# Output gate's columns of the input projection in two groups of four banks, recurrent heads' preparation beside them, convolutions beside k's and v's columns

## The reference

```python
x = x + 0.5 * swiglu(rmsnorm(x), w1_gate, w1_up, w1_down)      # D_FF = 5504
proj = rmsnorm(x) @ w_in                                       # 7192 columns
q_a, k_a, v_a, f_a, qk_m, v_m, o_m, i_m, f_m = split(proj)
y_a = rmsnorm(forgetting_attention(q_a, k_a, v_a, f_a, paged cache))       # 8 heads of 128
qk_c = silu(causal_conv(qk_m, conv_prev))                      # 4 taps, 2048 channels
h_m, C, n, m = mlstm(q_m, k_m, v_m, i_m, f_m, C0, n0, m0)      # 8 heads of 128
y_m = sigmoid(o_m) * rmsnorm(h_m)
x = x + concat(y_a, y_m) @ w_out
x = x + 0.5 * swiglu(rmsnorm(x), w2_gate, w2_up, w2_down)
```

## Time and profile before

| | |
|---|---|
| median of 3 runs | 2315.3 us (2314.76 to 2317.62) |
| profiled execution | 2320.72 us |
| its span | 2319.1 us |
| PE, share of the span | 2290.2 us, 99% |
| DVE, ACT, POOL | 1228.4 us (53%), 842.8 us (36%), 50.3 us (2%) |
| mean granted TensorE clock | 0.994 |
| chain of waits | PE 95%, DVE 3%, ACT 1% |

### The profile page before, as it was taken

How to read it: one execution, slowest core, us unless ns; L and a number is a source line. 1 busy time by engine, 2 the same in 40 slices (tenths; PEclk the granted TensorE clock), 3 DMA queues, 4 the chain that set the end, 5 groups by cost and what they waited for, 6 DMA issues and landing times.

```text
span 2319.1 us, 48002 instructions
## 1 busy us (share of the span) xinstructions
PE 2290.2 (99%) x17805; PEld 2246.8 (97%) x17805; DVE 1228.4 (53%) x1907; ACT 842.8 (36%) x1109; POOL 50.3 (2%) x84
## 2 busy tenths in 40 slices
PE   9999999999999999999999999999999999999998
PEld 8999999999999999887999989999999999999997
DVE  6554444355444455467456766755554434554443
ACT  4333333333333343334334433533333333333332
POOL 2000000000000010010000110000000000000000
PEclk9999999999999999999999999999999999999999
DMA  6555555555554444547445455455554445555443
GB/s 169 180 166 164 164 164 175 166 166 163 171 166 166 165 152 146 168 136 271 157 164 167 132 155 173 151 181 163 163 163 168 171 168 169 168 164 168 164 163 131
DMA packets 176901, 384.05 MB, mean 166 GB/s; under 512 B 19133, under 2 KB 44853, under 8 KB 176501
## 3 DMA queue, kind: packets, MB, share of 16 engines
q1 hardware_dynamic: 173888, 375.99, 50.4%
q0 software_dynamic: 2512, 5.57, 0.8%
q10 hardware_dynamic: 416, 1.32, 0.2%
HBM read 373.09 MB, written 9.70 MB: 165 GB/s over the span
## 4 chain that ended last, share of the span: by engine, by line
PE 95%; DVE 3%; ACT 1%; DMA 0%; issue 0%; SPq 0%; POOL 0%; ACTq 0%; DVEq 0%; POOLq 0%
PE ps L1788 30%; PE ps L1786 30%; PE ps L1787 29%; DVE w_lo L1010 1%; PE ps L2044 1%; DMA w_raw<-in_w_up 0%; ACT w_hi L632 0%; PE ps L2057 0%; PE ps L1856 0%; PE ps L1857 0%; PE ps L1863 0%; PE ps L1990 0%; PE ps L2337 0%; PE ps L1979 0%; PE ps L2245 0%
## 5 line engine op out<-in xcount | busy, mean ns | idle before, releaser
L1010 DVE TENSOR_TENSOR w_lo<-w_raw,w_hi 128x1024 fp32r<-128x1024 f32 (+2 forms) x698 | 789.7, 1172 | 983.9 <-ACT w_hi L632 982.5
L632 ACT CAST w_hi<-w_raw 128x1024 fp32r<-128x1024 f32 (+2 forms) x698 | 670.6, 1008 | 1290.3 <-PE ps L1788 1284.7
L1786 PE MATMUL ps<-x_hi,w_hi 128*128 128x288 f32 (+1 forms) x2752 | 813.0, 295 | 4.4 <-DVE w_lo L1010 2.6
L1788 PE MATMUL ps<-x_hi,w_lo 128*128 128x288 f32 (+1 forms) x2752 | 813.9, 296 | 0.0
L1787 PE MATMUL ps<-x_lo,w_hi 128*128 128x288 f32 (+1 forms) x2752 | 807.7, 293 | 0.0
L1786 PEld LDWEIGHTS ps<-x_hi,w_hi 128*128 128x128 f32 x2752 | 517.5, 188 | 6.3 <-DVE w_lo L1010 3.0
L1787 PEld LDWEIGHTS ps<-x_lo,w_hi 128*128 128x128 f32 x2752 | 521.2, 189 | 0.1
L1788 PEld LDWEIGHTS ps<-x_hi,w_lo 128*128 128x128 f32 x2752 | 516.5, 188 | 0.0
L1786 PE MATMUL ps<-hid_hi,w_hi 128*128 (+1 forms) x1376 | 405.6, 295 | 1.4 <-DVE X L1243 1.4
L1788 PE MATMUL ps<-hid_hi,w_lo 128*128 (+1 forms) x1376 | 407.0, 296 | 0.0
L1787 PE MATMUL ps<-hid_lo,w_hi 128*128 (+1 forms) x1376 | 403.8, 293 | 0.0
(11 more groups left out here) (487 smaller groups left out, 1438.1 us busy)
## 6 DMA issues: line engine op xcount, KB each, us to landing
w_raw<-in_w_down SPq DMA_DIRECT2D x178, 512.0 KB
w_raw<-in_w_gate SPq DMA_DIRECT2D x320, 256.0 KB
w_raw<-in_w_up SPq DMA_DIRECT2D x320, 256.0 KB
w_raw<-in_w_in SPq DMA_DIRECT2D x64, 512.0 KB
w_raw<-in_w_in SPq DMA_DIRECT2D x64, 384.0 KB
page<-in_cache_k SPq DMA_DIRECT2D x16, 512.0 KB, 4.6
w_raw<-in_w_out SPq DMA_DIRECT2D x16, 512.0 KB
w_raw<-in_w_gate SPq DMA_DIRECT2D x32, 192.0 KB
```

Source lines behind the costliest of these rows:

```text
L632: nc.scalar.copy(w_hi[:, slot, 0:width], w_raw[:, slot, 0:width]).then_inc(w_hi_ready, 1)
L1010: nc.vector.tensor_tensor(w_lo[:, slot, 0:width], w_raw[:, slot, 0:width], w_hi[:, slot, 0:width].bitcast(F32), ALU.subtract).then_inc(w_l ...
L1786: mm(out, hi, x_hi[:, k, :], start=first and pair == 0 and s == slots[0], stop=False)
L1788: ins = mm(out, lo, x_hi[:, k, :], start=False, stop=last and pair == 1 and s == slots[-1])
```

## The change

`in_m` keeps three groups (q, k, v). The gate's columns become `in_o`: two groups of four banks (0 to 3), each with four turns of 512 columns, so that banks 4 to 7 are free meanwhile. The preparation of the heads moves in between: on PE `beside_o1` and `beside_o2` put its pieces after given banks of given pairs ("steps" 0 to 7 of each group), on DVE and ACT a loop over 16 steps puts the copies and weights behind each `split_o`. Only the first scores stay behind the columns. The convolutions move one group up, beside k's and v's columns, in the turns of k's columns 0, 2, 3 and 3 of them. The memory of the heads is laid out anew so that what is written early lies where input blocks are used up: `O_HALF` and `O_MOST` are the marks at which four and six of the last group's eight pairs are done. `qw` is made by POOL instead of DVE, the sigmoid is split in two halves (the second after the first head's exponential), `kws` and `vws` move to `xt`, `Ws` to `counts`, and the first state is loaded at `O_MOST`.

```diff
-    mixer = [("in_a", 4, KD, KD, plain[:6]), ("in_m", 4, KD, KD, plain),
+    mixer = [("in_a", 4, KD, KD, plain[:6]), ("in_m", 3, KD, KD, plain),
+             ("in_o", 2, KD, KD, plain[:4]),
...
+    kws, vws = (xt[:, i, 0:H * SM].rearrange("p (h s) -> p h s", s=SM) for i in range(2))
+    C_ring = [C0[:, :, :], C1[:, :, :]] + [w_raw[:, i, :].rearrange("p (b e) -> p b e", b=NB) for i in (2, 3)]
...
+    O_HALF, O_MOST = ((IN_O.turn + IN_O.turns + n) * 2 + 2 for n in (2, 3))
...
+        first = (0, 0, 2, 5)[t] if t < 4 else 2 * t
+        return range(first, (0, 2, 5, 8)[t] if t < 4 else first + 2)
...
+            sp.wait_ge(w_used, O_MOST)
+            load_state(0)
...
+        pool.wait_ge(w_used, O_MOST)
+        for x in qw:
+            nc.gpsimd.memset(x[:, :, :], 0.0).then_inc(sem("km_ready"), 1)
...
-        split_groups(g, 2, UW)
+        split_groups(g, 1, UW)
         for t in range(2 * g.turns):
-            width = UW if t < 2 * g.turns - 1 else OUT_A.width
-            split_pair(g.turn + 2 * g.turns + (t + 1), 0, width)
-            conv_silu(2 * t)
-            conv_silu(2 * t + 1)
-            split_pair(g.turn + 2 * g.turns + (t + 1), 2, width)
...
+            width = UW if t < 2 * g.turns - 1 else IN_O.width
+            split_pair(g.turn + g.turns + (t + 1), 0, width)
+            for j in conv_tiles(t):
+                conv_silu(j)
+            split_pair(g.turn + g.turns + (t + 1), 2, width)
...
+        for step in range(16):
+            if step >= 1:
+                split_o(step + 1)
+            if step == 0:
...
+            if step in (1, 2):
+                for i in (2 * step - 2, 2 * step - 1):
+                    act.wait_ge(sem("vT_done"), 6 + i + 1)
+                    nc.scalar.copy(vmn[:, i // 2, 4 * (i % 2):4 * (i % 2) + 4, 0:HD],
...
+            if step in (4, 5):
+                conv_rows_copy(2 * step - 8)
+                conv_rows_copy(2 * step - 7)
+            if step == 9:
+                sigmoid(0)
+            if step == 10:
+                act.wait_ge(sem("ws_logits"), 1)
+                nc.scalar.activation(Ws, Ws, ACT.Exp).then_inc(sem("ws_exp"), 1)
+            if step == 15:
+                act.wait_ge(w_used, O_MOST)
+                for i in range(2):
+                    act.wait_ge(sem("kmsT_done"), i + 1)
+                    nc.scalar.copy(kms[:, i * 512:(i + 1) * 512], ps[:, 7 - 2 * i, :]).then_inc(sem("kms_ready"), 1)
+        split_o(17)
...
+        sigmoid(1)
...
+        for i in range(3):
+            width = UW if i < 2 else IN_O.width
+            if i == 0:
+                split_turns(g, g.turn, g.turns, UW)
             else:
                 for t in range(g.turns):
-                    conv((i - 2) * H + 2 * t)
-                    conv((i - 2) * H + 2 * t + 1)
-                    split_pair(g.turn + i * g.turns + (t + 1), 0, UW if (i, t) != (3, g.turns - 1) else OUT_A.width)
+                    for j in conv_tiles((i - 1) * g.turns + t):
...
+        def in_o_out(i):
+
+            for b in range(4):
+                wait_bank(dve, IN_O, IN_O.turn + i * IN_O.turns, IN_O.index + i, b)
+                nc.vector.tensor_tensor(om[:, 4 * i + b, :], ps[:, b, 0:T], rsx[:, :],
+                                        ALU.mult).then_inc(banks_free, 1 if b < 3 else 5)
...
+            if step == 7:
+                in_o_out(0)
...
+            if step == 12:
+                dve.wait_ge(w_used, O_HALF)
+                v_apart(0)
+                k_weighted(0)
+            if step == 13:
+                k_weighted(1)
+                v_apart(1)
+            if step == 14:
+                k_weighted(2)
+                k_weighted(3)
+        in_o_out(1)
+        split_o(17)
...
-        with pe.Fori(1, 4) as i:
+        with pe.Fori(1, 3) as i:
...
+        def beside_o1(step, b):
+
+            if step == 0 and b == 2:
+                s_spread()
+            if step == 1 and b < 2:
+                v_natural(b, 4 + b)
+            if step == 2 and b < 2:
+                pe.wait_ge(sem("s_all_ready"), b + 1)
+                v_natural(2 + b, 6 + b)
+            if step == 3 and b < 2:
+                pe.wait_ge(sem("vn_ready"), 6 + b + 1)
+                v_natural(4 + b, 4 + b)
...
+            if step == 4 and b == 0:
+                pe.wait_ge(sem("conv_last"), 4)
+                pe.wait_ge(sem("vn_ready"), 6 + 4)
+                conv_natural(0, 7)
+            if step == 4 and b == 1:
+                pe.wait_ge(sem("vmn_sample"), 1)
+                conv_natural(1, 4)
...
+            if step == 6 and b == 0:
+                pe.wait_ge(sem("km_ready"), H)
+                pe.wait_ge(sem("conv_rows_ready"), 1)
+                for h in range(H):
+                    ins = mm(ps[0:SM, 7, h * SM:(h + 1) * SM], ext[:, H + h, TP:T], ext[:, h, TP:T], start=True, stop=True)
+                ins.then_inc(sem("ws_scores"), 1)
...
+        def beside_o2(step, b):
+
+            if step == 2 and b == 0:
+                pe.wait_ge(sem("vws_ready"), 1)
+                pe.wait_ge(sem("ya_scaled"), 1)
+                by_sequence(vws, 0, 4, "vsT_done")
+            if step == 2 and b == 1:
+                pe.wait_ge(sem("conv_rows_ready"), 3)
+                by_sequence(vws, 1, 5, "vsT_done")
+            if step == 3 and b == 0:
+                pe.wait_ge(sem("conv_rows_ready"), 4)
+                k_natural(0, 6)
...
+            if step == 6 and b == 2:
+                pe.wait_ge(sem("v_seq_ready"), 2)
+                by_sequence(kws, 1, 5, "kmsT_done")
+
+        for i, beside in ((0, beside_o1), (1, beside_o2)):
+            for kt in range(IN_O.turns):
+                turn_products(IN_O, IN_O.turn + i * IN_O.turns, IN_O.index + i, kt, xm_hi, xm_lo, kt == 0,
...
-                pe.wait_ge(sem("kw_ready"), 2)
+                pe.wait_ge(banks_free, G_O * NBANK + 2)
...
+        pe.wait_ge(banks_free, NBANK + G_O * NBANK)
+        pe.wait_ge(sem("kw_ready"), 4)
+        pe.wait_ge(sem("kms_ready"), 2)
```

More of the change, by code:

```diff
@@ L922, in _ @@
-        for i in range(4):
-            act.wait_ge(sem("vT_done"), 6 + i + 1)
-            nc.scalar.copy(vmn[:, i // 2, 4 * (i % 2):4 * (i % 2) + 4, 0:HD],
-                           ps[:, i, :].rearrange("p (h d) -> p h d", h=4)).then_inc(sem("vn_ready"), 1)
-        nc.scalar.activation(om[:, :, :], om[:, :, :], ACT.Sigmoid).then_inc(sem("o_sigmoid"), 1)
-        for i in range(2):
-            act.wait_ge(sem("kmsT_done"), i + 1)
-            nc.scalar.copy(kms[:, i * 512:(i + 1) * 512], ps[:, 4 + i, :]).then_inc(sem("kms_ready"), 1)
+            width = UW if t < 2 * g.turns - 1 else IN_O.width
@@ new lines, in _, with sigmoid, conv_rows_copy @@
+            split_pair(g.turn + g.turns + (t + 1), 0, width)
+            for j in conv_tiles(t):
+                conv_silu(j)
+            split_pair(g.turn + g.turns + (t + 1), 2, width)
+        def sigmoid(i):
+            act.wait_ge(banks_free, NBANK + (IN_O.index + i + 1) * NBANK)
+            nc.scalar.activation(om[:, 4 * i:4 * i + 4, :], om[:, 4 * i:4 * i + 4, :], ACT.Sigmoid).then_inc(sem("o_sigmoid"), 1)
+        def conv_rows_copy(b):
+            act.wait_ge(sem("conv_rows_done"), b + 1)
+            nc.scalar.copy(conv_rows[:, b * 512:(b + 1) * 512], ps[0:27, (7, 4, 5, 6)[b], :]).then_inc(sem("conv_rows_ready"), 1)
@@ L945, in _ @@
         e_exp(0)
-        for b in range(4):
-            act.wait_ge(sem("conv_rows_done"), b + 1)
-            nc.scalar.copy(conv_rows[:, b * 512:(b + 1) * 512], ps[0:27, 2 + b, :]).then_inc(sem("conv_rows_ready"), 1)
-        act.wait_ge(sem("ws_logits"), 1)
-        nc.scalar.activation(Ws[:, :, :], Ws[:, :, :], ACT.Exp).then_inc(sem("ws_exp"), 1)
+        sigmoid(1)
         for h in range(H):
@@ L2163, in _, with s_spread @@
-        natural(lambda h, c, n: vm[:, h, c:c + n], 0, "vT_done")
-        pe.wait_ge(sem("rows_exp"), 3)
-        pe.wait_ge(sem("s_all_ready"), 1)
-        for a, row in enumerate((r_row, ws_row)):
-            for t, n in TT:
-                ins = tr(ps[0:n, 6, (3 * a + t) * H:(3 * a + t + 1) * H], row[:, t * P:t * P + n], ident[0:H, 0:H])
-        ins.then_inc(sem("nat_done"), 1)
-        def by_sequence(src, bank, made):
+        def s_spread():
+            pe.wait_ge(banks_free, NBANK + IN_O.index * NBANK)
+            pe.wait_ge(sem("s_rows_ready"), 1)
+            for b in range(2):
+                for j in range(4):
+                    ins = mm(ps[:, 6 + b, j * 96:(j + 1) * 96], sel[0:H, 4 * b + j, :].bitcast(F32), s_rows[:, :, :],
+                             start=True, stop=True)
+                ins.then_inc(sem("s_all_done"), 1)
@@ new lines, in v_natural, with rows_natural @@
+        def v_natural(i, bank):
+            (t, n), half = TT[i // 2], i % 2
+            for j in range(4):
+                ins = tr(ps[0:n, bank, j * P:(j + 1) * P], vm[:, 4 * half + j, t * P:t * P + n], ident[:, :])
+            ins.then_inc(sem("vT_done"), 1)
+        def rows_natural():
```

(17 more changed lines are left out.)

232 lines of the change are left out of this document (121 added, 111 removed).

## The result

The change makes the kernel slower: median 2322.6 us (2318.97 to 2324.97, 11 runs) against 2317.56 us of before (11 runs), ratio 1.0025 with a 95% interval of 1.0017 to 1.0033. Forecast was 2314.1 us. The profiled execution took 2322.17 us, its span is 2320.4 us. The first profiled execution of before, on which the prediction rests, took 2320.72 us, so the two profiles differ by 1.5 us and the medians by 5.0: a first hint that the profile of before was not a typical run.

The account below looks back on a forecast made before the run. PE, busy 99% of the span, bounds the kernel. Sum: -18.1 + 13.7 + 1.05 + 1.55 + 0.6 = -1.2 us; from 2315.3 this gives 2314.1 us, own range 2311.5 to 2316.5, with rivals 2310.7 to 2317.9.

Parts of the forecast that it names:

- The block removed: PE's small matmuls between the input projection's last dense matmul and the first head, except first scores: 18.1 us removed.
- 4.4 us would be won: Block removed less the same work between dense matmuls: 0.9 us gaps, about 3.3 slow clock, the rest spacing.
- The same work mixed: Transposes, selections, spreads, sample scores and rows between dense matmuls cost PE 13.7 us (13.2 to 15.5).
- 0.36 a burst: Four transposes between dense matmuls lengthen PE's way by 0.36 us; 14 such bursts make 5.0 us.
- Stalls A, B and the gate: PE waits: 1.05 us before k's seventh pair, 1.55 at v's first matmul, 0.6 before the first scores.
- Queues: Moved state loads cost nothing, with DMA idle up to the first head; POOL's weighted queries finish 3 us before the heads.
- Table switches: Halved sigmoid adds two 1.28 us ACT loads: cost 0, margin 0.75; rival with drains: 2316.1 us, chance 0.03.
- The clock in the mixed stretch: PE's clock taken as full while small matmuls run among dense ones; a fall would lose the 3.3 us again.
- Rival 3 with two falls: Clock falls twice in the mixed stretch or after a stall: +5.6 us, 2320.9 us, chance 0.06.

Follow-up runs that it names:

- stores of m early: The changed kernel with only the two stores of m moved, issued beside q's columns some 180 us earlier; median 2319.6 us, ratio to before 1.0019.
- second trace of before: The kernel before, unchanged, run and traced again; this trace took 2314.8 us, the runs have median 2318.0 us, ratio 1.0005.
- early silus: The changed kernel with the first silu of k's third and fourth turns ahead of ACT's cast; median 2319.8 us, ratio to before 1.0014.
- three edits: The changed kernel with early silus, POOL's four stores behind the first head's gating, and two DVE bank copies between its splits; median 2322.2 us, ratio to before 1.0014.
- spread cut: As three edits, with PE's spread of `s_rows` in two bursts of eight instead of one of sixteen; median 2322.7 us, ratio to before 1.0018.

## Why the prediction was wrong, step by step

- **The block removed.** 18.1 us hold as read in that one trace, but 3.4 of them were slow clock. The fall was indeed spared in some traces (none in the mixed stretch with the stores of m early), yet the mean clock loss is 11.2 against 10.4 to 11.4. At full clock the block is 14.7 us. *This is the first failed step*: "4.4 us would be won: 0.9 of gaps, about 3.3 of slow clock" took a length from a single execution whose slow share was unusual, and moved the result to the median as if that were common to all runs. In the second trace of before the fall at the block is 3.41 us long and costs 1.7, not 3.4.
- **The same work mixed.** 13.7 was forecast, 15.2 measured: transposes 6.1 for 5.0 (14 bursts of 0.44), selections 4.74 for 4.45, spreads 2.14 for 2.1, scores and the last spread 1.64 for 1.65, rows 0.59 for 0.5. *The second failed step*, a size: 0.36 a burst leaves out the 0.09 that the first dense matmul behind it loses. 15.2 lies inside the range of 13.2 to 15.5 that the text gave. With it the mixture costs more than the block at full clock.
- **Stalls A, B and the gate.** Forecast 1.05, 1.55 and 0.6; measured 1.01, 1.44 and 0.56, with 0.2 of spacing behind the first two. Right in place, cause and size; the early silus and the convolutions moved alone confirm the cause.
- **Queues.** *The third failed step, 1.83 us*: the text priced SP's state loads and POOL's queries, and left POOL's four stores out. `store` stands behind `conv_rows_ready`, which the change makes 41 us earlier; the trace of before shows the last store taking 7.4 us to land for 0.2 KB. It was harmless there because the first four states were loaded beside the block and no further load was issued until it had landed.
- **Table switches.** No wait of PE for the weights of head 1: nothing to pay, as taken. ACT's timeline in the changed kernel:

```profile
1332.13 1.28 ACT L946 ACT_TABLE_LOAD   x1
1333.42 1.17 ACT L946 ACTIVATE om<-om 128x1152 f32<-128x1152 f32 x1
```

  The sigmoid starts as the load ends. The 1.38 us that the Trainium skill ("ScalarE: Activation LUTs", What ACT_TABLE_LOAD costs) adds for a drain did not reach PE here.
- **The clock in the mixed stretch.** Of the changed kernel and its nine variants four traces have a fall there (the change, early silus, three edits, spread cut), of the four traces of before's order all do. By the rule of the Trainium skill ("TensorE: Matmul & The Clock Gate", Part 4) transposes don't count as activity; the runs do not decide on it, since the fall began behind the spreads of `s_rows`, ahead of the first transposes of v. Rival 3 with two falls, 2320.9, is the nearest time that was written down, but its mechanism is not what made the time.

With the measured sizes the forecast's own sum reads -14.7 + 15.2 + 2.65 + 1.83 + 0.56 = +5.5 of engine part; the traces say +5.35, the medians +5.0. Of the 6.7 us between the forecast's -1.2 and this, 3.4 are the first failed step, 1.5 the second and 1.8 the third. A further 2.3 us between 2314.1 and the measured 2322.6 are no step of the sum: the forecast started from 2315.3, the median of three runs, and eleven runs of before have 2317.56.

## What to carry to other kernels

Small matmuls set among dense ones are not free on an engine that is 99% busy: they cost their own time plus what the next dense matmul loses, so such a move can win only idle gaps (0.9 us here), and here the small matmuls took 15.2 us mixed against 13.8 in the block at full clock without its gaps. Before a block is dissolved, ask what else hangs on its results: here four stores came 41 us earlier, out of a time without loads into the weight traffic. And where a term is a clock fall, take it from the mean clock of many runs, never from one trace.
